# Hybrid attention block on one core: how weight sums are spread over the DMA queues, and the order of the first down jobs

## What is computed

```python
h = rms_norm(x, ln1_g);  proj = h @ w_in
o_a = mla_mixer(...)     # multi-head latent attention
o_b = nsa_mixer(...)     # compressed, selected and window branches, mixed by gates
mix = concatenate([rms_norm(o_a, grp_norm_mla), rms_norm(o_b, grp_norm_nsa)])
x = x + mix @ w_o
h2 = rms_norm(x, ln2_g)
x = x + square(relu(h2 @ w_up)) @ w_down
```

## Time and profile before

| | us |
|---|---|
| median of 3 runs (lowest, highest) | 688.23 (687.5, 688.56) |
| the profiled execution | 686.12 |
| its span, first to last instruction | 684.3 |
| TensorE busy | 643.7 |
| VectorE busy | 514.1 |
| ScalarE busy | 361.9 |
| GpSimd busy | 137.2 |
| DMA, mean rate | 205 GB/s |

### The profile page before, as it was taken

The page is one execution under the profiler, slowest core; times in us unless marked ns, Lnnn a source line. Parts: engine busy times, 40 slices in busy tenths (PEclk is TensorE's granted clock), DMA queues, the critical chain, the costliest instruction groups (busy, mean ns, idle before and its releaser), DMA issues.

```text
span 684.3 us, 11701 instructions
## 1 busy us (share of the span) xinstructions
PE 643.7 (94%) x4189; PEld 569.7 (83%) x4189; DVE 514.1 (75%) x943; ACT 361.9 (53%) x728; POOL 137.2 (20%) x197
## 2 busy tenths in 40 slices
PE   8999999999979943999899999999999999999998
PEld 6999788887668832888799999999998868788887
DVE  5655765689757813889788588988879898999784
ACT  5564674478856610765645644434433454656660
POOL 2436654343521500221100000000001010000000
PEclk9999999999989985999999999999999999999999
DMA  7481639899989999598003478778776779546772
GB/s 289 145 305 65 247 136 302 191 316 309 273 190 312 312 302 286 183 247 188 1 8 117 124 217 216 196 207 232 196 205 165 199 206 237 170 151 198 225 236 102
DMA packets 33419, 140.39 MB, mean 205 GB/s; under 512 B 4584, under 2 KB 4968, under 8 KB 32402
## 3 DMA queue, kind: packets, MB, share of 16 engines
q1 hardware_dynamic: 23522, 104.70, 43.8%
q0 software_dynamic: 9696, 34.88, 26.9%
q10 hardware_dynamic: 144, 0.07, 0.0%
HBM read 137.48 MB, written 65.06 MB: 296 GB/s over the span
## 4 chain that ended last, share of the span: by engine, by line
PE 70%; DMA 14%; DVE 8%; ACT 3%; issue 3%; POOL 1%; SPq 0%; DVEq 0%; ACTq 0%
PE bank L2014 11%; PE bank L2016 10%; PE bank L2015 10%; PE bank L2431 6%; PE bank L2433 6%; PE bank L2432 6%; DMA x<-x 6%; PE bank L2034 5%; DMA bias_ct<-bias_by_distance 2%; DMA raw<-w_down 2%; PE bank L2209 2%; PE bank L2248 2%; DMA raw<-weights 2%; PE bank L2266 2%; PE bank L2361 1%
## 5 line engine op out<-in xcount | busy, mean ns | idle before, releaser
L1307 DVE TENSOR_TENSOR w_lo<-raw,w_hi 128x1024 fp32r<-128x1024 f32 (+3 forms) x70 | 80.5, 1159 | 24.3 <-ACT w_hi L921 24.3
L2014 PE MATMUL bank<-w_hi,act_hi 128*128 128x512 f32 (+3 forms) x224 | 90.5, 404 | 1.7 <-DVE act_lo L1321 0.9
L921 ACT ACTIVATE w_hi<-raw 128x1024 fp32r<-128x1024 f32 (+3 forms) x70 | 68.6, 994 | 40.8 <-DMA raw<-w_pairs 28.9
L2015 PE MATMUL bank<-w_lo,act_hi 128*128 128x512 f32 (+3 forms) x224 | 80.2, 358 | 0.0
L2016 PE MATMUL bank<-w_hi,act_lo 128*128 128x512 f32 (+3 forms) x224 | 80.1, 358 | 0.0
L1057 ACT ACTIVATE p_buf<-s_buf,stats 128x128 f32<-128x128 f32 (+3 forms) x96 | 53.8, 561 | 39.3 <-PE bank L2034 25.1
L2034 PE MATMUL bank<-consts,p_buf 128*128 128x128 f32 x248 | 45.8, 283 | 23.2 <-DVE pt_buf L1482 21.8
L834 POOL DMA_DIRECT2D down_sums<-w_down x32 | 26.5, 933 | 197.9 <-PE bank L2433 148.1
L2014 PE MATMUL bank<-w_hi,s_all 128*128 128x512 f32 x140 | 54.9, 392 | 1.6 <-DVE w_lo L1895 1.5
L2034 PEld LDWEIGHTS bank<-consts,p_buf 128*128 128x128 f32 x248 | 31.8, 154 | 29.0 <-issue 26.1
L2016 PE MATMUL bank<-w_hi,s_all 128*128 128x512 f32 x140 | 54.5, 389 | 0.0
(11 more groups left out here) (308 smaller groups left out, 1822.2 us busy)
## 6 DMA issues: line engine op xcount, KB each, us to landing
down_sums<-w_down SPq DMA_DIRECT2D x32, 512.0 KB, 17.3
down_sums<-w_down POOLq DMA_DIRECT2D x32, 512.0 KB, 7.2
raw<-down_sums SPq DMA_DIRECT2D x32, 512.0 KB, 4.3
up_sums<-w_pairs SPq DMA_DIRECT2D x28, 512.0 KB, 6.9
up_sums<-w_pairs POOLq DMA_DIRECT2D x28, 512.0 KB, 17.9
raw<-up_sums SPq DMA_DIRECT2D x28, 512.0 KB, 4.5
raw<-weights SPq DMA_DIRECT2D x26, 512.0 KB, 7.2
raw<-w_down SPq DMA_DIRECT2D x16, 512.0 KB, 4.2
```

Source lines behind the costliest of these rows:

```text
L921: ins = act.activation(hi[:, 0:width], raw[:, n % RAW, 0:width], ACT.Copy)
L1307: ins = dve.tensor_tensor(lo[:, 0:width], raw[:, n % RAW, 0:width], hi[:, 0:width].bitcast(F32), ALU.subtract)
L2014: pe.matmul(dst, a_h, w_h, start=start, stop=False, skip_group_check=onto)
L2015: pe.matmul(dst, a_h, w_l, start=False, stop=False, skip_group_check=onto)
```

## The change

- `COPY_AT`: one copy behind each of pieces 9 to 24, two behind 25 to 28, then 3, 2, 2, three behind each of 32 to 40, and two behind 41 (before: one behind 9 to 20, two to 24, three to 28, four behind 29, three to 35, two to 38).
- GpSimd: from sum 8 on the up adds are issued in twos, each two behind one step of the norms, the last behind `ln2_rsqrt(0)`. All 32 down adds come after that: three for two pairs (sum k behind the `A` product of pair 2k // 3), the last eleven behind `m2` jobs 0 to 6.
- `S_TMP` is 6 instead of 4; the two new buffers lie over the second pair of halves of `D`'s weights.
- Down jobs: the low half of job 1's weights is made after `cross_out(13)` rather than before; job 3 comes with job 2 ahead of the last diagonal; each difference is made earlier than before, one job after the other.
- ScalarE splits `B` of the last pair ahead of `keep(12)`.
- The second half of tile 3's rows is kept at unit 61 instead of 59, its low half made at 62 instead of 60.

```diff
-SLOTS, S_RING, S_TMP = RING + 3, 8, 4
+SLOTS, S_RING, S_TMP = RING + 3, 8, 6
...
-COPY_AT = [n for n, times in [(n, 1) for n in range(9, 21)] + [(n, 2) for n in range(21, 25)] + [(n, 3) for n in range(25, 29)]
-           + [(29, 4)] + [(n, 3) for n in range(30, 36)] + [(n, 2) for n in range(36, 39)] for _ in range(times)]
+COPY_AT = [n for n, times in [(n, 1) for n in range(9, 25)] + [(n, 2) for n in range(25, 29)] + [(29, 3), (30, 2), (31, 2)]
+           + [(n, 3) for n in range(32, 41)] + [(41, 2)] for _ in range(times)]
...
+KEEP_AT = {3: (58, 61), 2: (66, 67)}
...
         s_tmp = [half[:, 2 * j:2 * j + 2, :] for half in spare for j in range(2)]
+        s_tmp += [place(f"s_tmp{h}", 512, at=at).rearrange("p (j s) -> p j s", j=2) for h, at in enumerate((r_diff + 4096, r_down + 32768))]
...
-            add_up(8)
+            add_up(8, 2)
...
-            add_up(12)
+            add_up(10, 2)
...
             for t in range(3):
                 mix_row_of(0, t)
-            add_up(16)
+            add_up(12, 2)
             pool.wait_ge(*dve_step.at("kc_ss"))
             rsqrt("kc", kc_rs[0:64, :], kc_ss[0:64, :], HD)
             mix_row_of(0, 3)
-            add_up(20, 8)
+            add_up(14, 2)
             mix_row_of(1, 3)
-            for k in range(4):
-                add_down(k)
+            add_up(16, 2)
             mix_row_of(1, 2)
-            for k in range(4, STEPS):
-                add_down(k)
+            add_up(18, 2)
...
             ln2_rsqrt(3)
+            add_up(20, 2)
             mix_row_of(1, 1)
             ln2_rsqrt(2)
+            add_up(22, 2)
             ln2_rsqrt(1)
             mix_row_of(1, 0)
+            add_up(24, 2)
             ln2_rsqrt(0)
-
-            for k in range(STEPS, len(SUM_JOBS)):
-                j = k - STEPS
-                pool.wait_ge(*(dense_done.at(("A", j)) if j < PAIRS else job_used.at(JOB_AT["m2", (j - PAIRS) // 2])))
+            add_up(26, 2)
+
+            for k in range(len(SUM_JOBS)):
+                p, i = 2 * k // 3, (k - 3 * PAIRS // 2) * 2 // 3
+                pool.wait_ge(*(dense_done.at(("A", p)) if p < PAIRS else job_used.at(JOB_AT["m2", i])))
                 add_down(k)
...
-                    if u - 1 - LN2_AT[t][2] in (0, 1):
-                        keep_rows(t, u - 1 - LN2_AT[t][2])
+                    if u in KEEP_AT[t]:
+                        keep_rows(t, KEEP_AT[t].index(u))
...
                 if p == PAIRS - 1:
                     job_hi(1)
+                if p == PAIRS - 2:
+                    split_hi(PIECE_AT["B", p + 1])
                 keep(p)
                 if p + 2 < PAIRS:
                     diff_hi(p + 2)
-                if p + 1 < PAIRS:
                     split_hi(PIECE_AT["B", p + 1])
...
-                    if n - N_MLA in (LN2_AT[t][2] + 2, LN2_AT[t][2] + 3):
-                        ln_lows(t, "ln2", [n - N_MLA - LN2_AT[t][2] - 2])
+                    if n - N_MLA - 1 in KEEP_AT[t]:
+                        ln_lows(t, "ln2", [KEEP_AT[t].index(n - N_MLA - 1)])
...
                 m, i = JOBS[d]
                 if m == "m5":
                     weight_difference(i)
+                factor_lo_of(d)
+                weight_lo_of(d)
+
+            def factor_lo_of(d):
+
                 hi, lo = s_halves(d)
                 dve.wait_ge(*factor_hi.at(JOBS[d]))
                 dve.tensor_tensor(lo, factor(d), hi.bitcast(F32), ALU.subtract).then_inc(*factor_lo.mark(JOBS[d]))
+
+            def weight_lo_of(d):
+
+                m, i = JOBS[d]
                 hi, lo = job_halves(d)
...
                 elif before >= -2:
-                    dve.wait_ge(*pair_out.at(("diagonal", PAIRS + before)))
+                    dve.wait_ge(*dense_done.at(("D", PAIRS - 1)))
+                elif before >= -4:
+                    dve.wait_ge(*pair_out.at(("diagonal", PAIRS + 2 + before)))
...
                 if p == PAIRS - 1:
                     factor_of("m5", 0)
-                    job_lo(1)
+                    weight_difference(0)
+                    factor_lo_of(1)
                 cross_out(p)
...
+            weight_lo_of(1)
             job_lo(2)
+            job_lo(3)
             diagonal_out(PAIRS - 1)
             squared(("diagonal", PAIRS - 1), diagonal(PAIRS - 1), ALU.min)
-            factor_of("m1", 1)
-            for d in range(3, len(JOBS)):
+            for m in ("m1", "m2", "m5"):
+                factor_of(m, 1)
+            for d in range(4, len(JOBS)):
...
                 job_lo(d)
-                if m == "m2" and i:
-                    factor_of("m5", i)
                 if m == "m2" and i == 2:
                     row_diffs(STEPS - 1)
-                if m == "m5" and 0 < i < STEPS - 1:
-                    factor_of("m1", i + 1)
-                if m == "m1" and i < STEPS - 1:
-                    factor_of("m2", i + 1)
+                if d < 4 * STEPS - 4 and m != "m1":
+                    factor_of({"m2": "m1", "m5": "m2", "m3": "m5"}[m], i + 1)
```

## The result

The changed kernel takes 662.62 us (median of 4 runs, 659.59 to 665.09) against 687.87 for the kernel before: a ratio of 0.963, 95% interval 0.9589 to 0.9671. Forecast were 656.5 us and 651.5 to 667. Time and direction were right and the time lies in the range, but 6 us of the 31.6 forecast did not come; in the profiled executions it is 23.5 of 31.6.

What follows compares the result with a forecast made beforehand. The prediction took TensorE, busy 643.7 of 684.3 us, as the bound, its two long stops being DMA queueing. Gains 5.4 + 1.7 + 1.0 + 19.8 + 1.5 + 0.7 + 1.5 = 31.6 us gave 656.5 us, range 651.5 to 667.

Steps and rivals of the forecast that it cites:

- `bias_ct` stop: TensorE's 5.4 us wait for the `bias_ct` loads, queued behind adds and copies; claimed to go entirely, gain 5.4 us.
- `w1`: TensorE's wait for a weight load 1.0 us late; fewer copies and adds around it, gain 1.0 us.
- The reload: Second reload of `x`, TensorE stop 21.8 us: subtraction left 2.9, queue sum 0 to 2; took 2.0, gain 19.8.
- the clock behind the reload: Half-clock stretch after the stop at the reload of `x`: a stop of 2 leaves the clock up, gain 1.5 us.
- slack is 4.3 us against 2.8: cost 0: Pair stage: an even pair's second add delays the load of `P` up to 2.8 us, within 4.3 us slack.
- rival (b): Pair stage: two adds cost `P` 5.5 us, 1.2 beyond slack, seven times, 8.4 us: 665 us; chance 0.12.
- the average, 8.7, fits in 10.08: Pair stage: average DMA work of 8.7 us per pair fits in the pair's 10.08 us.
- The last pair: VectorE's low half of job 1 moves behind `cross_out(13)`, removing a TensorE wait: gain 0.7 us.
- The down jobs: Six difference buffers end the ping-pong waits, 1.9 us in three stops: gain 1.5 us.
- Arrival order (a): Reload of `x`: engines serve transfers as issued, so adds issued later don't delay it: 670 us; chance 0.08.
- (c): At 190 and in the norms: the stops' cover is gone, ScalarE nearly full, no clock gains: 660 us; chance 0.12.
- The prediction's own signs: Right if: no `bias_ct` wait, `x` wait under 5 us, reload some 20, clock full, pairs 100%, down-job waits under 1.

Runs made afterwards that it cites:

- e6: The changed kernel with six copies moved from in front of the reload of `x` to behind it: 654.25 us, ratio 0.9529.
- e7: The changed kernel with two up adds (14 and 15), issued just behind the reload of `x`, moved to the next norm: 655.27 us, ratio 0.9537.
- e10: The changed kernel itself, run again: 659.67 us, ratio 0.9582 to the kernel before.
- e4: The changed kernel with the down adds issued as in the kernel before: 672.25 us, ratio 0.9798.
- e9: e8 with four early down adds instead of eight, then one behind each pair: 653.01 us, ratio 0.948.
- e5: The changed kernel with eight down adds early, behind the last up adds, then one behind each pair: 666.17 us, ratio 0.9691.
- e8: The changed kernel with the edits of e5, e6 and e7 together: 659.43 us, ratio 0.9594.
- e3: The kernel before with the compute edits alone (six difference buffers, down-job order, `B13` split, later keep): 683.41 us, ratio 0.997.
- e2: The kernel before with only the up adds issued in twos, as in the changed kernel: 662.99 us, ratio 0.9663.
- e11: The changed kernel without its compute edits, with all of its DMA schedule: 662.69 us, ratio 0.9623.
- e12: The changed kernel with the edits of e6 and e7 together: 655.6 us, ratio 0.9516.

## Why the prediction was right or wrong

**Right: what bounds it.** The two long stops were DMA backlog, and taking work from in front removed them. The `bias_ct` stop came out at 5.4 us, as forecast, and `w1` at 1.3 for 1.0. Behind `bias_ct` 1.6 us of half clock were won, but TensorE lost 0.5 of them again right away.

**The reload: right mechanism, the size off by 2.1 us** (17.7 for 19.8). The prediction's subtraction gave a stop of 2.9 us (248.6 less 245.7). It took 2.0 instead, because adding up the new queue was said to give 0 to 2. It does not: 5 + 13 + 4 transfers and 4 adds are 22 x 1.50 + 4 x 2.77 = 44.1 us, which from 203.2 ends at 247.3, the same landing as by the subtraction. That choice is 0.9 of the 2.1 us. The rest is small: SyncE began at 196.98 and the reload was used at 241.67, 44.7 us later and not 44.1; and TensorE ran dry 41.9 us after that beginning, not 42.5.

**Wrong: the clock behind the reload.** "I take it that a stop of 2 leaves the clock up": it was a stop of 4.1, and 3.4 us at the 1.2 GHz level followed it, where the old stop had 3.0 us of it left for work. The gain (1.6 us) came only in e6 and e7, where the stop is gone.

**Wrong: "slack is 4.3 us against 2.8: cost 0".** This is rival (b), in part. The cost of the second add was sized about right: it made the loads of `P` 1.5 to 3.9 us later than the 3.3 us of the odd pairs, most of them under the 2.8. What failed is the slack, 3.1 and not 4.3, since VectorE's work on `P` was left out, and the step "the average, 8.7, fits in 10.08": that holds for the DMA work, but not for the loop from load to VectorE to the next load, in which a late load makes the next one late. TensorE lost 4.6 us in the pair stage of the first trace with the clock (3.7 and 0.9), and its stops for `a_all` alone, the last pair's with them, sum to 1.4 us in e10. Under one add a pair (e4 and e9, and e5 and e8 after pair 0) there are none. The rival's price of 8.4 us was too high: it takes all seven even pairs, and two or three stop.

**The last pair.** Forecast -0.7, measured +0.1. In e3 the edit gives its 0.7. With two adds in an even pair the last `B` comes late too (ScalarE waits 2.80 us for it at 487.76), and as its split now stands ahead of `keep(12)`, that copy and the sums behind it are late as well, which gives the 0.7 back. In e9 there is no stop.

**The down jobs** gave 2.0 for 1.5 in this trace and 1.2 in e3, by the mechanism named. That the new order has two short stops of its own at the start (0.5 us each) was not foreseen, and e10's stop of 1.6 us shows that the gain can be lost again.

**What was missed and cost nothing here:** that the down adds had to leave the norms. The prediction valued GpSimd's issue time there and not its waits for earlier sums, behind which the memset and the second norm are queued. e4 puts 15.0 us of its trace on it.

**The rivals.** Arrival order (a) is refuted by e2 and e7. (c), that other engines had used the standstills, did not happen: all of the 5.4 came.

**The prediction's own signs.** Of those for "right", the `bias_ct` wait is gone and the DMA share of the two-add pairs is 0.85 (376 to 478 us). These were missed: VectorE waited 5.87 us for `x` and not under 5, the reload took 24.9 us and not some 20, the clock fell at 242.8, and the down jobs' waits sum to 1.3 us and not under 1. The pair stage was not at 100% (150.67 of 153 us). The sign of rival (b), waits for `a_all` in even pairs, was there.

Left open: why the runs of the change spread over 5 us. The two traces differ in the pair stage and in the third down step, but only these two were seen. Also not tried was a version in which `add_down` issues without its wait.

## What to carry to other kernels

Price a DMA backlog by adding up all the work that shares the engines until the late transfer must land, on every queue and also what is issued after it; here 1.5 us for a half-megabyte load or copy and 2.8 for an add held to within 1 us. Background transfers belong where nothing urgent is loaded, in doses below the slack of the next load: four adds in a gap were free, eight cost 6 us. A slack is read on every engine of the path, and it holds once: where each load waits for work that the last one started, compare the whole round, load and work, with the bottleneck's period. And before moving them in an engine's stream, look for waits inside the issuing helper and what stands behind them.

## What the runs showed of the hardware

A stop of TensorE as short as 1.9 us (at 398.86) was followed by a stretch at the 1.2 GHz level:

```profile
399.90:403.30 3.40, 3.40 (x18) 3.40 (x17) 3.40 (x5) 2.06 (x3) 0.00 (x0) 0.50 0.30 99
```

TensorE was busy in all of it and lost 1.4 us. A longer stop is not needed for such a stretch. In the kernel before, one began at 329.5, with no stop above 0.6 us in the 7 us ahead of it, in which TensorE was busy for 6.03:

```profile
322.50:329.50 7.00, 6.03 (x45) 5.14 (x43) 4.85 (x19) 5.89 (x20) 1.98 (x4) 1.00 0.00 1
329.50:332.90 3.40, 3.40 (x15) 3.11 (x15) 3.24 (x13) 2.23 (x10) 0.00 (x0) 0.50 0.00 0
```

The trace after, e10 and e9 have none there, e11 and e12 have one (at 303.1 and 300.5), so it comes and goes between executions of nearly the same work.

The two adds that were issued 2.7 us behind the reload delayed it by 6.0 us with the copies in front of it (e7) and by 5.5 without six of them (e12 against e6).
